# Experts' outputs returned to their tokens by rows in HBM and indirect transfers instead of by spreading matrices

## The chip, the cores and the metric

The program runs on one core of one Trainium2 chip. The metric is the device time of one execution in microseconds (us), as the median of several runs. The engines are TensorE (PE; its weight loads are shown as PEld), VectorE (DVE), ScalarE (ACT), GpSimd (POOL) and SyncE (SP), which here does nothing but issue the transfers of weights; 16 DMA engines move the data.

## The reference, cut to what matters

The program is two transformer blocks in float32 for 256 tokens of width 1024. The first block has two layers, and the feed-forward part of its second layer is a mixture of eight experts, of which each token takes two. That is the part that the change is about:

```python
def moe_swiglu(h, router, wg, wu, wd):            # h: 256 tokens x 1024, 8 experts, d_ff 3584
    logits = (xt @ router).astype(jnp.float32)
    top_logit, top_e = lax.top_k(logits, TOP_K)   # TOP_K = 2
    gate = jax.nn.softmax(top_logit, axis=-1)
    ...
    def expert_block(args):
        xb, e = args
        return swiglu(xb, wg[e], wu[e], wd[e])    # (silu(x@wg) * (x@wu)) @ wd

    ys = lax.map(expert_block, (xs, blk_e)).reshape(n_slots, d)
    ys = ys * slot_gate[:, None].astype(ys.dtype)
    out = jax.ops.segment_sum(ys, slot_tok, num_segments=n_tok + 1)[:n_tok]
    return out.reshape(b, s, d)
```

So each token's result is the sum of two experts' rows, each times its gate, and it is added to the residual x. The second block then starts with a norm of x.

## The kernel before, in words

The whole program is written out by hand, one instruction stream for each engine, with semaphores between them. A token block is 128 tokens, so x is a tile `xv` of 128 partitions by two token blocks (q = 0, 1) by 1024 columns, which stays in SBUF.

**Ahead of the experts** (`moe_sparse` in the streams of TensorE and VectorE). The router's logits give `route`, each token's rank within its experts, and `logit[:, 66:70]`, its two gates. When no expert has over CAP = 96 tokens (else `moe_dense` runs, which did not happen here), VectorE builds 16 pieces of a 0/1 matrix `pick` (L2170), and TensorE multiplies x by it (L1156): 16 banks of 384 columns, each the gathered tokens of four experts for one chunk of 128 columns of x. VectorE takes each bank to `big` (L2191) and copies the first expert's tokens to `hcur` (L2194). In between it builds a second set of 16 pieces, `weigh` (L2176): for each expert, token by slot, with the gate as its value. Behind the 16 gathering banks TensorE transposes `weigh` in four banks of four (L825), and VectorE copies them out (L2198) into `back`, slot by token. The two PSUM banks `pt` are used in turn, and a bank is filled again only when VectorE has emptied it.

**One expert.** Its weights come as 46 tiles: gate and up in two parts of 512x4 and 384x4 columns (tiles "g", "u", part 0 and 1, eight tiles each), then down in two halves of the output (h = 0, 1), seven tiles each. SyncE issues them in that order into ten slots (six of `ring`, and `xc`, `biasb` and two halves of `prob`), each when TensorE has freed its slot, which makes it run up to ten tiles ahead. A group of 96 tokens is three groups of 32, and TensorE's array is used as four column strips of 32, the fourth taking a piece of the others' work; each instruction of L1098 (gate, up) and L1124 (down) handles one strip. At the end of each half of down ScalarE copies partitions of the result (L1690) and VectorE adds the fourth strip's part to them (`add_sides`, L2232 to L2237), which gives `ysum[:, h, :]`, 96 slots by 512 columns.

**Back to the tokens.** `spread_out(h, nth)` (L1141 to L1146) multiplies `backcur`, the current expert's 128x256 piece of `back`, by `ysum[:, h, :]`: two matmuls of 128x512, one for each token block, into the banks `po` and `pada`. VectorE adds both to x (`add_spread`, L2206). There are 17 of them: the one of h = 0 stands inside the same expert's second half of down, behind its second tile; the one of h = 1 stands in the next expert's first gate part, behind its second tile (the first expert has one too, of zeros); the last expert's stands behind the loop, between the turns of the context.

**Behind the experts.** The second block's first steps are TensorE's turning of the context tokens (`turn_context`, L1137), VectorE's `take_context` (L2160), TensorE's first projection of the context, "c4" (L852), then the turning of x by `turner` (L833), the projection "c0" (L852) and the ones of x. The norm of x needs `x_ready`: ScalarE squares x (L1551), VectorE and ScalarE make the root, and VectorE makes `turner` (L1831), on which L833 waits.

GpSimd has nothing in the experts' stage. It waits for a free slot to prepare a table for the last attention (L743 on), which is used far later.

## Time and profile before

| | us |
|---|---|
| median of 3 runs (2952.91 to 2957.2) | 2956.97 |
| profiled execution, its own time | 2956.31 |
| its span, from the first to the last instruction | 2954.5 |

In the profiled execution TensorE is busy 94% of the span, its weight loads 59%, VectorE 43%, ScalarE 15%, GpSimd 2%. The chain of waits that ended last lies on TensorE for 88% of the span, on VectorE for 7%, on "issue" for 2%, on DMA, GpSimd and ScalarE for 1% each. The span in 40 slices of 74 us looks so, with the busy share in tenths, the clock that was granted to TensorE (9 is full, 2.4 GHz; the other level is 1.2 GHz), and the rate of the DMA:

```
PE   7889999989799999999999998899979999988998
PEclk9889999969799999999999999999999999999999
GB/s 269 187 172 143 172 168 175 200 172 101 171 338 378 358 395 376 377 385 362 392 382 353 395 223 83 67 114 172 171 72 114 171 172 128 61 79 47 163 166 99
```

The stretch at 338 to 395 GB/s is the experts' stage. A busy share says which engine works, not which one is waited for; that is read from timelines and waits in the stretch that is asked about. In a timeline a row merges instructions of one line that follow each other; "x" is how many, and what stands in square brackets is the idle time ahead and who ended it. A float32 matmul is recorded as two passes, so counts on TensorE are twice the number of instructions.

### The profile page before, as it was taken

The numbers are of one execution on the slowest core, as the hardware profiler recorded it, in microseconds if no ns is written. First come the engines' busy times: TensorE is split into PE (matmuls) and PEld (weight loads), VectorE is DVE, ScalarE is ACT, GpSimd is POOL, SyncE is SP. The second block draws the span as 40 slices with busy tenths as digits, with TensorE's granted clock in tenths as the row PEclk, the third lists the DMA queues.
The fourth block names the chain that finished last, engine by engine and source line by source line (L and its number), as shares of the span: only waits on it lengthen the run. The fifth ranks groups of instructions, "written<-read, shape, count | busy, mean of one in ns | idle before, by whom it ended". The sixth has DMA issues, their size and how long they took to land.

```text
span 2954.5 us, 49536 instructions
## 1 busy us (share of the span) xinstructions
...
## 2 busy tenths in 40 slices
PE   7889999989799999999999998899979999988998
...
PEclk9889999969799999999999999999999999999999
...
GB/s 269 187 172 143 172 168 175 200 172 101 171 338 378 358 395 376 377 385 362 392 382 353 395 223 83 67 114 172 171 72 114 171 172 128 61 79 47 163 166 99
DMA packets 309636, 629.79 MB, mean 213 GB/s; under 512 B 14841, under 2 KB 197505, under 8 KB 292912
## 3 DMA queue, kind: packets, MB, share of 16 engines
...
## 4 chain that ended last, share of the span: by engine, by line
PE 88%; DVE 7%; issue 2%; DMA 1%; POOL 1%; ACT 1%; DVEq 0%; POOLq 0%; SPq 0%; ACTq 0%
PE pacc L1024 13%; PE pt L852 10%; PE pacc L1098 10%; PE pt L1098 7%; PE pt L1024 6%; PE pacc L1062 5%; PE pacc L1124 5%; PE pt L1124 5%; PE pacc L965 5%; PE po L1098 3%; PE pt L1062 3%; PE pt L1003 2%; PE pt L1361 2%; DVE prob L1914 2%; PE pacc L875 1%
## 5 line engine op out<-in xcount | busy, mean ns | idle before, releaser
L2218 DVE TENSOR_TENSOR gateb<-kT,pt 128x512 f32<-128x512 f32 (+1 forms) x32 | 19.9, 621 | 452.4 <-PE pt L1098 451.7
L852 PE MATMUL pt<-ring,hT 128*128 128x256 f32 (+1 forms) x896 | 206.6, 391 | 7.9 <-ACTq L1572 3.9
L852 PEld LDWEIGHTS pt<-ring,hT 128*128 128x128 f32 x896 | 174.6, 205 | 37.0 <-issue 13.9
L1098 PE MATMUL pacc<-ring,bigc 128*32 128x512 f32 (+1 forms) x1920 | 190.3, 550 | 4.4 <-issue 3.2
L1024 PE MATMUL pacc<-probT,prob 128*128 128x128 f32 x1440 | 170.6, 275 | 0.0
L1024 PEld LDWEIGHTS pacc<-probT,prob 128*128 128x128 f32 x1440 | 165.6, 192 | 0.0
L1098 PEld LDWEIGHTS pacc<-ring,bigc 128*32 128x32 f32 x1920 | 63.1, 110 | 128.2 <-issue 128.2
L1098 PE MATMUL pt<-ring,bigc 128*32 128x512 f32 (+1 forms) x1280 | 138.3, 550 | 0.0
L1124 PE MATMUL pacc<-ring,bigc 128*32 128x512 f32 x864 | 137.9, 595 | 0.0
L1062 PE MATMUL pacc<-prob,chunks 128*128 128x512 f32 x282 | 136.3, 592 | 0.0
L1124 PE MATMUL pt<-ring,bigc 128*32 128x512 f32 x1056 | 126.6, 593 | 0.0
L2028 DVE TENSOR_TENSOR prob<-ring 128x512 f32<-128x512 f32 x86 | 59.5, 692 | 153.8 <-PE pacc L1024 107.1
L1609 ACT ACTIVATE prob<-prob,den 128x256 f32<-128x256 f32 (+3 forms) x192 | 99.2, 518 | 156.5 <-DVEq L1942 152.6
L965 PE MATMUL pacc<-ring,hT 128*128 128x512 f32 x256 | 111.3, 593 | 0.9 <-DVEq L2014 0.9
L852 PE MATMUL pt<-ring,prob 128*128 128x256 f32 x448 | 103.0, 390 | 5.5 <-DVEq L2163 4.0
L2455 DVE SCALAR_TENSOR_TENSOR bigc<-big,convw,bigc 128x256 f32<-128x256 f32 x240 | 100.3, 480 | 4.4 <-DVE hid L2501 0.5
L825 PE MATMUL pt<-const,prob 128*128 128x128 f32 (+1 forms) x448 | 71.1, 303 | 31.4 <-DVEq L1802 28.0
L1682 ACT ACTIVATE kT<-pacc 128x512 f32<-128x512 f32 (+1 forms) x48 | 26.1, 545 | 502.0 <-PE pacc L1098 502.0
L852 PEld LDWEIGHTS pt<-ring,prob 128*128 128x128 f32 x448 | 86.8, 195 | 19.8 <-issue 6.1
L1062 PEld LDWEIGHTS pacc<-prob,chunks 128*128 128x128 f32 x282 | 53.6, 190 | 67.4 <-issue 67.4
L1098 PEld LDWEIGHTS pt<-ring,bigc 128*32 128x32 f32 x1280 | 41.6, 110 | 82.1 <-issue 82.1
L1024 PE MATMUL pacc<-hT,ring 128*128 128x128 f32 x736 | 89.7, 275 | 0.0
...
## 6 DMA issues: line engine op xcount, KB each, us to landing
ring<-in_moe_w_down SPq DMA_DIRECT2D x80, 1024.0 KB, 14.0
ring<-in_w_gate_up SPq DMA_DIRECT2D x66, 1024.0 KB, 5.1
ring<-in_w_ada SPq DMA_DIRECT2D x48, 1024.0 KB, 5.7
ring<-in_moe_w_gate SPq DMA_DIRECT2D x48, 1024.0 KB, 5.4
ring<-in_moe_w_up SPq DMA_DIRECT2D x48, 1024.0 KB, 14.5
ring<-in_w_down SPq DMA_DIRECT2D x33, 1024.0 KB, 4.9
ring<-in_moe_w_gate SPq DMA_DIRECT2D x32, 768.0 KB, 9.4
ring<-in_moe_w_up SPq DMA_DIRECT2D x32, 768.0 KB, 6.5
```

The source lines that it names most:

```text
L825: return pe.transpose(dst, src, ident[0:n, 0:n])
L852: ins = pe.matmul(t[:, q * 256:q * 256 + n], src[:, k, q * P:q * P + P], w[:, k, 0:n], start=(k == 0), stop=(k == KC - 1))
L965: ins = pe.matmul(pacc[:, o:o + 512], src[:, kc, q * P:q * P + P], w[:, k, h * 512:h * 512 + 512], start=(kc == 0), stop=(kc == KC - 1))
L1003: ins = pe.matmul(pt[cc][:, j * S + lo:j * S + lo + P], tiles[j][:, k, cc * P:cc * P + P], half(k, q), start=(k == 0), stop=(k == KC - 1))
L1024: ins = pe.matmul(bank_[:, o:o + P], left(k), right(k), start=(k == 0), stop=(k == 3))
L1062: ins = pe.matmul(down_bank[m][:, 0:512], left[m], right[m], start=(g == 0), stop=(g == groups - 1), skip_group_check=True)
L1098: ins = pe.matmul(((X, Y, Z) if kind == "g" else up_bank)[r][32 * j:32 * j + 32, 0:w], hcurv[:, kc, 32 * g:32 * g + 32], moe_view(tile_)[: ...
L1124: ins = pe.matmul(banks[0 if j < 3 else i][32 * j:32 * j + 32, :], actT[:, f, 32 * g:32 * g + 32], w[:, f - 4 * t, :], start=(t == 0 and ( ...
L1361: ins = pe.matmul(t[:, h * S + lo:h * S + hi], w[:, k, h * P:h * P + P], hTv[:, k, lo:hi], start=(k == 0), stop=(k == KC - 1))
L1609: act.activation(prob[:, o:o + b.nk], prob[:, o:o + b.nk], ACT.Exp, scale=-1.0, bias=den[:, 8 + (i % 4) * 4 + j:9 + (i % 4) * 4 + j], accu ...
L2028: go(ve.tensor_tensor(s1, a21, a22, ALU.add))
L2455: go(ve.scalar_tensor_tensor(out=y[:, cc, :], in0=src, scalar=wk, in1=y[:, cc, :], op0=ALU.mult, op1=ALU.add))
```

## The change

There are no spreading matrices any more: `weigh`, `back`, `backcur`, the transposes, `spread_out` and `add_spread` are gone. `add_sides` now copies three strips rather than two, and adds three. When half h of expert e is in `ysum`, GpSimd writes its 96 rows of 512 columns to a tensor in HBM, `expert_rows` (768 rows of 1024), and waits for that transfer before it allows the next copy into `ysum` (`y_free`, which starts at 2, so that the two halves alternate). VectorE works out the row that each token has with each of its experts (`find_rows`, six small steps behind the first expert's tokens). Behind the last write GpSimd issues four indirect transfers, one for each token block and choice, each of 128 rows of 4 KB, into `big`, and VectorE multiplies each by its gate and adds it to x (four passes over 128x1024), behind `take_context`. `x_ready` is told one token block at a time.

```diff
@@ -739,6 +736,21 @@
             for dst, src in pos_loads:
                 pool.dma_start(dst, src, allow_slow_non_contiguous=True).then_inc(positions, 16)
             pool.sem_inc(slot_free[7], 1)
+            pool.sem_inc(y_free, 2)
+            for e in range(NE):
+                for h in range(2):
+                    pool.wait_ge(y_copied, e * 2 + h + 1)
+                    pool.wait_ge(y_ready, e * 6 + 9 + 3 * h)
+                    pool.dma_start(expert_rows[e * CAP:e * CAP + CAP, 512 * h:512 * h + 512], ysum[0:CAP, h, :])\
+                        .then_inc(y_written, 16)
+                    pool.wait_ge(y_written, 16 * (2 * e + h + 1))
+                    pool.sem_inc(y_free, 1)
+            pool.wait_ge(rows_wanted, 1)
+            for q in range(QT):
+                for c in range(2):
+                    j = 2 * q + c
+                    pool.indirect_dma_start(big[:, j * D:j * D + D], None, expert_rows,
+                                            bass.IndirectOffsetOnAxis(ap=top_i[:, j:j + 1], axis=0)).then_inc(rows_back[q], 16)
...
 
-            def spread_out(h, nth):
-
-                pe.wait_ge(spread_taken, nth)
-                for q, bank_ in enumerate((po, pada)):
-                    ins = pe.matmul(bank_[:, :], backcur[:, q * P:q * P + P], ysum[:, h, :], start=True, stop=True)
-                ins.then_inc(spread_done, 1)
-
...
@@ -1157,33 +1162,19 @@
                                             pick[:, q, half * 4 * CAP:(half + 1) * 4 * CAP],
                                             start=(q == 0), stop=(q == QT - 1))
                         ins.then_inc(filled, 1)
-                pe.wait_ge(weighed_out, 1)
-                for e in range(0, NE, 2):
-                    t, filled, uses, emptied = bank()
-                    pe.wait_ge(emptied, uses)
-                    for k in range(4):
-                        ins = transpose(t[:, k * P:k * P + P], weigh[:, e + k // 2, k % 2, :])
-                    ins.then_inc(filled, 1)
...
                 for e in range(NE):
                     pe.sem_inc(wide_filled, 14)
                     pe.wait_ge(h_current, e + 1)
-                    pe.wait_ge(y_ready, e * 4 + 2)
-
-                    def last_spread():
-                        pe.wait_ge(y_ready, e * 4 + 4)
-                        spread_out(1, e * 2 + 1)
+                    pe.wait_ge(y_ready, e * 6 + 3)
...
-                    def nothing():
-                        pass
-
-                    gate_up(e, "g", 0, None, [nothing, last_spread])
-                    pe.wait_ge(spread_taken, e * 2 + 2)
+                    gate_up(e, "g", 0, None, [])
+                    pe.wait_ge(y_ready, e * 6 + 6)
...
@@ -1199,16 +1190,12 @@
                         down(e, 0, t, (X, Y, Z))
                     down(e, 1, 0, (pt[0], pt[1], turned), freed(("d", 0, 6, 0)))
                     down(e, 1, 1, (pt[0], pt[1], turned))
-                    pe.wait_ge(back_current, e + 2)
-                    pe.wait_ge(y_ready, e * 4 + 6)
-                    spread_out(0, e * 2 + 2)
                     for t in range(2, 7):
                         down(e, 1, t, (pt[0], pt[1], turned))
                     pe.drain().then_inc(freed(("d", 1, 6, 0)), 1)
                 turn_context(0, (0, 1))
                 turn_context(1, (0,))
-                pe.wait_ge(y_ready, NE * 4 + 4)
-                spread_out(1, NE * 2 + 1)
+                pe.wait_ge(y_ready, NE * 6 + 6)
                 turn_context(1, (1,))
...
@@ -1687,7 +1674,8 @@
                         act.wait_ge(wide_taken, e * 14 + (j + 1))
                     for h in range(2):
                         act.wait_ge(y_done, e * 2 + (h + 1))
-                        act.activation(ysum[:, h, :], (X, pt[0])[h][:, :], ACT.Copy).then_inc(y_copied, 1)
+                        act.wait_ge(y_free, e * 2 + (h + 1))
+                        act.activation(ysum[0:CAP, h, :], (X, pt[0])[h][0:CAP, :], ACT.Copy).then_inc(y_copied, 1)
...
             def moe_sparse():
                 g = colA[:, COL["ffn_norm_g"] + KC:COL["ffn_norm_g"] + 2 * KC]
                 for e in range(NE):
@@ -2170,20 +2172,11 @@
                         go(ve.tensor_scalar(pick[:, q, e * CAP:e * CAP + CAP], cst("iota")[:, 0:CAP], r,
                                             den[:, 2 + q:3 + q], ALU.is_equal, ALU.mult))
                 tell(picked)
-                for e in range(NE):
-                    for q in range(QT):
-                        r = route[:, 16 + q * NE + e:17 + q * NE + e]
-                        go(ve.tensor_scalar(weigh[:, e, q, :], cst("slots"), r,
-                                            logit[:, 80 + q * NE + e:81 + q * NE + e], ALU.is_equal, ALU.mult))
-                tell(weighed_out)
                 go(ve.memset(ysum[:, 1, :], 0.0))
                 go(ve.memset(stage, 0.0))
-                go(ve.memset(backcur, 0.0))
                 settle()
-                ve.sem_inc(back_current, 1)
-                ve.sem_inc(y_ready, 4)
+                ve.sem_inc(y_ready, 6)
                 ve.sem_inc(turned_taken, 1)
-                ve.sem_inc(spread_taken, 1)
...
@@ -2192,22 +2185,7 @@
                                             t[:, 0:4 * CAP].rearrange("p (e n) -> p e n", e=4), g[:, k:k + 1], None, ALU.mult))
                         tell(emptied)
                 ve.tensor_copy(hcur, gathered[:, 0, :]).then_inc(h_current, 1)
-                for e in range(0, NE, 2):
-                    t, filled, uses, emptied = bank()
-                    ve.wait_ge(filled, uses)
-                    go(ve.tensor_copy(back[:, e * S:(e + 2) * S], t[:, :]))
-                    tell(emptied)
-
-                def add_spread(h, nth):
-
-                    ve.wait_ge(spread_done, nth)
-                    for q, bank_ in enumerate((po, pada)):
-                        o = x[:, q * D + 512 * h:q * D + 512 * h + 512]
-                        ins = ve.tensor_tensor(o, o, bank_[:, :], ALU.add)
-                        if q == 0:
-                            ins.then_inc(y_shifted, 1)
-                        else:
-                            ins.then_inc(spread_taken, 1)
+                find_rows()
...
@@ -2229,17 +2207,17 @@
                 def add_sides(e, h, banks):
 
                     ve.wait_ge(y_done, e * 2 + (h + 1))
-                    ve.tensor_copy(yside[32:64, h, :], banks[1][96:128, :]).then_inc(y_shifted, 1)
-                    ve.tensor_copy(yside[64:96, h, :], banks[2][96:128, :]).then_inc(y_shifted, 1)
+                    for g in range(3):
+                        ve.tensor_copy(yside[32 * g:32 * g + 32, h, :], banks[g][96:128, :]).then_inc(y_shifted, 1)
                     ve.wait_ge(y_copied, e * 2 + (h + 1))
                     ve.wait_ge(y_shifted, e * 6 + (3, 6)[h])
-                    for lo in (32, 64):
+                    for lo in (0, 32, 64):
                         ve.tensor_tensor(ysum[lo:lo + 32, h, :], ysum[lo:lo + 32, h, :], yside[lo:lo + 32, h, :], ALU.add)\
                           .then_inc(y_ready, 1)
 
                 def expert(e, last=False):
-                    add_spread(1, e * 2 + 1)
-                    ve.tensor_copy(backcur, back[:, bass.ds(e * S, S)]).then_inc(back_current, 1)
+                    if last:
+                        ve.sem_inc(rows_wanted, 1)
...
@@ -2255,7 +2233,6 @@
                         ve.tensor_copy(hcur, big[:, bass.ds((e + 1) * EW, EW)]).then_inc(h_current, 1)
                     take_turned(e, 5)
                     add_sides(e, 0, (X, Y, Z))
-                    add_spread(0, e * 2 + 2)
                     if last:
                         context_scales()
                     add_sides(e, 1, (pt[0], pt[1], turned))
@@ -2264,13 +2241,19 @@
                     expert(e)
                 expert(NE - 1, last=True)
                 take_context(0)
-                add_spread(1, NE * 2 + 1)
                 take_context(1)
-                ve.wait_ge(y_shifted, NE * 6 + 1)
-                ve.wait_ge(spread_taken, NE * 2 + 2)
-                ve.sem_inc(x_ready, QT)
+                for q in range(QT):
+                    ve.wait_ge(rows_back[q], 32)
+                    for c in range(2):
+                        w = logit[:, 66 + 2 * c + q:67 + 2 * c + q]
+                        link(ve.scalar_tensor_tensor(out=xv[:, q, :], in0=big[:, (2 * q + c) * D:(2 * q + c + 1) * D],
+                                                     scalar=w, in1=xv[:, q, :], op0=ALU.mult, op1=ALU.add))
+                    ve.sem_inc(x_ready, 1)
+                ve.sem_inc(vector_chain, 32)
+                chain[0] += 32
 
```

(Left out: names of semaphores and buffers that come or go, the constant `slots`, `find_rows` itself, and the counts that `moe_dense` keeps in step.)

In the order of TensorE's stream, the seam of two experts reads so before (the last tiles of the second half of down, then the first gate part; `chunks` holds `ysum`, `kT` holds `backcur`, `bigc` the tokens and the hidden values):

```order
L1124 MATMUL pacc<-ring,bigc 32x512
L1124 MATMUL pt<-ring,bigc 32x512 x11
L1124 MATMUL pacc<-ring,bigc 32x512
L1098 MATMUL pacc<-ring,bigc 32x512 x24
L1145 MATMUL po<-chunks,kT 128x512
L1145 MATMUL pada<-chunks,kT 128x512
L1098 MATMUL pacc<-ring,bigc 32x512 x48
L1098 MATMUL pacc<-xc,bigc 32x512 x12
L1098 MATMUL pacc<-biasb,bigc 32x512 x12
```

and now:

```order
L1136 MATMUL pacc<-ring,bigc 32x512
L1136 MATMUL pt<-ring,bigc 32x512 x11
L1136 MATMUL pacc<-ring,bigc 32x512
L1110 MATMUL pacc<-ring,bigc 32x512 x72
L1110 MATMUL pacc<-xc,bigc 32x512 x12
L1110 MATMUL pacc<-biasb,bigc 32x512 x12
L1110 MATMUL pt<-prob,bigc 32x512 x8
L1110 MATMUL po<-prob,bigc 32x512 x4
```

The pair that writes `po` and `pada` is gone, and the gate's tiles on both sides of it follow each other. The other pair of an expert, behind the second tile of down's second half, goes in the same way.

VectorE ahead of the first expert before (`probT` is `weigh`, `kT` is `back`):

```order
L2170 TENSOR_SCALAR qT<-const,route,den 128x96 x16
L2176 TENSOR_SCALAR probT<-const,route,logit 128x128 x16
L2179 MEMSET chunks 128x512
L2180 MEMSET qT 128x512
L2181 MEMSET kT 128x256
L2191 TENSOR_SCALAR big<-pt,colA 128x4x96 x16
L2194 COPY bigc<-big 128x768
L2198 COPY kT<-pt 128x512 x4
```

and now:

```order
L2172 TENSOR_SCALAR qT<-const,route,den 128x96 x16
L2175 MEMSET chunks 128x512
L2176 MEMSET qT 128x512
L2184 TENSOR_SCALAR big<-pt,colA 128x4x96 x16
L2187 COPY bigc<-big 128x768
L2158 TENSOR_TENSOR work<-const,logit 128x32
L2160 TENSOR_TENSOR work<-work,route 128x32
L2161 TENSOR_REDUCE work<-work 128x4
L2162 SCALAR_TENSOR_TENSOR work<-logit,work 128x4
L2164 TENSOR_SCALAR work<-work 128x4
L2165 CAST top_i<-work 128x4
```

The 16 pieces of `weigh` between `pick` and the gathering banks are gone, and behind the copy of the first expert's tokens the four copies of `back` are replaced by the six steps of `find_rows`.

VectorE behind the last expert before, from its last `add_sides` on (`prob` is the context's tile):

```order
L2232 COPY work<-pt 32x512
L2233 COPY work<-pacc 32x512
L2237 TENSOR_TENSOR chunks<-chunks,work 32x512 x2
L2160 TENSOR_SCALAR prob<-pacc,gsc,mod 128x128 x8
L2206 TENSOR_TENSOR x<-x,po 128x512
L2206 TENSOR_TENSOR x<-x,pada 128x512
L2160 TENSOR_SCALAR prob<-pacc,gsc,mod 128x128 x8
```

and now, with GpSimd's new instructions below it:

```order
L2211 COPY work<-pt 32x512 x2
L2211 COPY work<-pacc 32x512
L2215 TENSOR_TENSOR chunks<-chunks,work 32x512 x3
L2148 TENSOR_SCALAR prob<-pacc,gsc,mod 128x128 x16
L2249 SCALAR_TENSOR_TENSOR x<-big,logit,x 128x1024 x4
```

```order
L737 DMA posi<-in_positions 15x1
L744 DMA expert_rows<-chunks 96x512 x16
L752 DMA big<-expert_rows,top_i 128x1024 x4
L755 MEMSET biasb 16x889
L758 DMA biasb<-in_na_rpb 16x7x31
L761 ISA
```

The adds to x stood between the two halves of `take_context`; now they are four wider passes behind both, and they read `big`, which the four indirect transfers fill. Those stand behind the 16 writes in GpSimd's queue, and its old work (`biasb`) behind them.

## Rows read from the trace of the kernel before

**Rows 1.** Stages of the span: us, busy time of each engine, granted clock, DMA share, GB/s.

```profile
747.00:802.50 55.50, 37.45 (x122) 24.92 (x121) 29.25 (x87) 1.86 (x3) 0.00 (x0) 0.71 0.42 174
802.50:1738.00 935.50, 932.29 (x9064) 310.36 (x9064) 129.28 (x258) 116.30 (x189) 3.86 (x3) 1.00 0.97 370
```

**Rows 2.** Timeline, TensorE, the start of one expert.

```profile
1153.57 5.36 PE L1098 MATMUL pacc<-ring,bigc 128*32 128x512 f32 x48 [0.44 <-issue]
1158.85 1.12 PE L1145 MATMUL po<-chunks,kT 128*128 128x512 f32 x2
...
1160.77 10.51 PE L1098 MATMUL pacc<-ring,bigc 128*32 128x512 f32 x96
```

**Rows 3.** Groups by line in the experts' stage: the spreading matmuls.

```profile
L1145 PE MATMUL po<-chunks,kT 128*128 128x512 f32 x34 | 19.1, 645 | 0.0
```

**Rows 4.** DMA issues at 1156.4 to 1157.0 and at 1207 to 1208, us to landing.

```profile
ring<-in_moe_w_up SPq DMA_DIRECT2D x1, 1024.0 KB, 16.9
...
prob<-in_moe_w_up SPq DMA_DIRECT2D x1, 768.0 KB, 5.1
```

**Rows 5.** Stretches of five microseconds inside one expert.

```profile
1120.00:1125.00 5.00, 5.00 (x47) 1.51 (x43) 1.17 (x4) 0.00 (x0) 0.00 (x0) 1.00 1.05 387
...
1135.00:1140.00 5.00, 5.00 (x36) 1.46 (x28) 1.00 (x2) 0.00 (x0) 0.00 (x0) 1.00 0.76 222
1140.00:1145.00 5.00, 5.00 (x49) 1.59 (x52) 1.28 (x2) 0.00 (x0) 0.00 (x0) 1.00 0.67 228
...
1160.00:1165.00 5.00, 5.00 (x42) 1.33 (x45) 1.49 (x3) 0.00 (x0) 0.00 (x0) 1.00 1.01 424
```

**Rows 6.** Timeline of TensorE and VectorE ahead of the first expert.

```profile
769.40 4.29 PE L1156 MATMUL pt<-qT,x 128*128 128x384 f32 x8 [6.13 <-DVEq L1802]
769.43 4.19 DVE L2176 TENSOR_SCALAR probT<-const,route,logit 128x128 f32<-128x128 f32 x16 [0.15 <-DVE qT L2170]
...
776.37 21.39 PE L1156 MATMUL pt<-qT,x 128*128 128x384 f32 x56 [2.69 <-DVEq L1802]
...
788.76 0.62 DVE L2191 TENSOR_SCALAR big<-pt,colA 128x384 f32<-128x384 f32 x1 [0.67 <-PE pt L1156]
...
798.56 0.56 DVE L2194 COPY bigc<-big 128x768 f32<-128x768 f32 x1
...
802.54 1.02 PE L1098 MATMUL pacc<-ring,bigc 128*32 128x512 f32 x5 [1.22 <-DVEq L1802]
```

**Rows 7.** Two stretches at the lower clock.

```profile
776.00:779.00 3.00, 2.63 (x4) 1.51 (x5) 0.88 (x2) 0.00 (x0) 0.00 (x0) 0.50 0.00 0
...
1749.00:1751.00 2.00, 2.00 (x6) 1.53 (x6) 0.67 (x4) 1.31 (x4) 0.00 (x0) 0.50 0.44 135
```

**Rows 8.** Timeline behind the last expert.

```profile
1738.09 0.69 DVE L2232 COPY work<-pt 32x512 f32<-32x512 f32 x1 [7.83 <-PE pacc L1124]
...
1747.92 1.06 ACT L1551 ACTIVATE prob<-x 128x1024 f32<-128x1024 f32 x1 [9.14 <-DVEq L2271]
1747.94 8.83 PE L852 MATMUL pt<-ring,prob 128*128 128x256 f32 x32 [3.99 <-DVEq L2163]
...
1749.89 0.29 DVE L1831 TENSOR_SCALAR turner<-const,den 128x128 f32<-128x128 f32 x1 [0.36 <-ACT den L1557]
...
1756.61 3.73 PE L833 MATMUL pacc<-turner,x 128*128 128x128 f32 x32
...
1760.18 7.07 PE L852 MATMUL pt<-ring,prob 128*128 128x256 f32 x32
```

**Rows 9.** DMAs issued by GpSimd, KB each, us to landing.

```profile
biasb<-skew_scratch POOLq DMA_DIRECT2D x64, 64.0 KB, 2.4
skew_scratch<-biasb POOLq DMA_DIRECT2D x1, 3556.0 KB, 38.8
...
biasb<-in_na_rpb POOLq DMA_DIRECT2D x1, 13.6 KB, 5.2
```

**Rows 10.** VectorE groups by shape: one pass over 1024 columns.

```profile
L2578 DVE SCALAR_TENSOR_TENSOR bigc<-pt,bigc 128x1024 f32<-128x1024 f32 x2 | 2.4, 1224 | 4.9 <-PE pt L1377 4.9
```

42 lines of the change are left out of this document (28 added, 14 removed).

## The prediction, made before the changed kernel was run

> **What bounds the kernel now.** I read the stages first, then the timeline of each place that the change touches, then the DMA. In the experts' stage, from 802.5 to 1738.0, TensorE is busy 932.29 of 935.5 us at the full clock, 2.4 GHz [rows 1]. Eight experts in 935.5 us are 116.9 us each, and what TensorE does there is the stage. VectorE (129 us) and ScalarE (116 us) have long pauses in it, so what they gain or lose inside the stage costs nothing by itself. Ahead of it, from 747.0 to 802.5, TensorE is busy 37.45 of 55.5 us at a mean clock of 0.71 [rows 1]: there it waits, for VectorE. The one resource near TensorE in the experts' stage is the DMA, with a share of 0.97 [rows 1]. So three questions decide: what TensorE's stream gets shorter by, whether the weights still come in time, and what the way through HBM costs behind the last expert, where nothing of the experts' stage covers it.
>
> **The change part by part.**
>
> *The spreading matmuls.* In the first gate part a pair goes from 1158.85 to the next tile's first matmul at 1160.77: 1.92 us. The two tiles before it take 5.28 us from 1153.57, where the four behind it take 10.51 with the end of the last one in it, so 5.2 by their rate [rows 2]; the array changes from four strips to one block and back, and I take 2.0 us for each pair. The group by line has 34 records of the `po` half, at two for each matmul 17 pairs [rows 3]. 16 stand inside the stage: 16 x 2.0 = 32 us. The seventeenth stands behind the loop, where VectorE sets the pace; it is worth nothing.
>
> *What hides the rest inside the stage.* VectorE has four passes of 128x512 less per expert and four of 32x512 more, ScalarE copies 96 partitions rather than 128 at the same length: both in their pauses. TensorE now waits for both halves' `y_ready` ahead of the second gate-or-up part, 20 us behind the last tile of down, where three copies and three adds of 0.7 us are long done (one copy is in [rows 8]). ScalarE's wait for `y_free` is for a write issued over 90 us earlier. If a write took so long, the next y copy would wait and TensorE with it; the slowest transfer of GpSimd's queue, 3556 KB, took 38.8 us [rows 9].
>
> *The weights.* An expert is now 116.9 - 4.0 = 112.9 us long. Does the DMA deliver 44.0 MB in that? Its 14 tiles of down (14.7 MB) come at 387 GB/s, where the share is full, those of gate and up (29.4 MB) at 424, of which I take 418: 37.9 + 70.2 = 108.1 us [rows 5]. The new writes are 0.39 MB per expert, 1.0 us at 387. 109.1 of 112.9 us: it fits, with 3.8 us left. The queue says the same. The longest time to landing is 16.9 us, for the tile issued at 1156.5, that is 1173.4; it is the eleventh tile of the expert that starts at 1153.57, and with 5.36/2 = 2.6 us per tile and the pair TensorE comes to it at 1181 [rows 2, 4]. That leaves 8 us, and 6 without the pair. 50 us later a tile lands in 5.1 us [rows 4], so the queue has run dry again and nothing adds up from expert to expert. And from 1135 to 1145 the share is 0.76 and 0.67 at 222 and 228 GB/s [rows 5], since SyncE waits there for slots. So I cost the weights at nothing.
>
> *Ahead of the first expert.* VectorE builds `weigh` from 769.43 to 773.62 and then clears three buffers; TensorE fills two banks by 773.69 and is idle for 2.69 us until 776.37, since nobody empties them [rows 6]. Behind that pause its clock is 1.2 GHz, 0.50 at 776 to 779 [rows 7]. The 14 other banks take 21.39 us, to 797.76, of which the later ones go at 0.62 + 0.67 = 1.29 us each [rows 6]. Now VectorE is ready after two clearings, before the first bank is full, and TensorE does not pause. At the full clock the 14 banks are 14 x 1.29 = 18.1 us, from 773.7 to 791.8: 6.0 us earlier. The copy to `hcur` ended at 799.12, 1.36 us behind the gathers' end, and the first expert started only at 802.54, since the transposes and four copies of `back` stood between; now it can start 0.3 us behind the copy, at 793.4. Sum: 802.5 - 793.4 = 9.1 us. If the clock falls all the same, the pause (2.7) and the wait behind the copy (3.1) are what is won, 5.8 us. I take 9.1, since the fall came behind a pause that goes. `find_rows` is six steps on 32 columns, some 1.5 us, and VectorE is next wanted some 40 us later.
>
> *Behind the last expert.* The last tile is done at 1738.09, on the clock of before. Three copies and three adds of 0.7 us: `ysum` is complete at 1742.4 rather than 1741.0. `take_context` then needs no pause for the adds to x (two of 0.68), so c4 starts as before, at 1747.94, and ends at 1756.6, when TensorE wants x turned. In the kernel before `turner` was made from 1749.89 on, so x came with 6 us to spare [rows 8]. What it now takes:
> the write, 192 KB, issued at 1742.5. The trace has 2.4 us for 64 KB and 5.2 for 13.6 KB while weights were streaming [rows 9]; the streaming goes on to about 1750, where the share is down at 0.44 [rows 7], so 5.5: 1748.1.
> The four gathers of 512 KB. None is in the trace. From below: 2.1 MB at 387 GB/s are 5.4 us, and behind them the 2.4 us of a small transfer. From above: at the rate of GpSimd's only large transfer, 3556 KB in 38.8 us, they take 22.9 us [rows 9]. The weights' burst is over by 1750, and rows of 4 KB are long, so I go near the lower end, with 1.2 us on GpSimd for each: block 0 at 1754.5, block 1 at 1756.9.
> The four passes: 1.22 us for a SCALAR_TENSOR_TENSOR of 1024 columns [rows 10], all four ahead of the norm in VectorE's order. Block 0 is added by 1757.0, block 1 by 1759.5; then the root and `turner`, as before 1.1 us behind the first squares. TensorE turns x at 1760.7 rather than 1756.6: 4.1 us. TensorE's pause of 3.99 us at 1744 was followed by a clock of 0.50 at 1749 to 1751 [rows 7, 8], and c4's 32 records took 8.83 us where c0's 32 took 7.07 [rows 8]; the new pause is as long, so I take another 1.7. Sum: 5.8 us lost. Behind it everything is as before: the context's head "c4" and the projection "c0" move with it.
>
> The page DMA: Bandwidth & Descriptors of the Trainium skill (Anatomy of one DMA) gives a GpSimd transfer 2.0 us plus its bytes at 436 GB/s. This trace agrees for the 64 KB (2.15 against 2.4) and not for the 13.6 KB under load (2.03 against 5.2). By that rule x would be turned in time and this loss would be nothing; that is my third case below, whose numbers come from the rows.
>
> *Sum*, against the profiled execution's 2956.3: - 32 - 9.1 + 5.8 = - 35.3, so 2921.0. The median shown is 0.7 above that execution; I leave that in the range.
>
> **The rivals.**
> 1. *The weights become the bound.* For it: a DMA share of 0.97 in the stage [rows 1], of which by this count only 3.5 us per expert are free, and the writes take 1.0 of them. Then an expert gets shorter by 2.5 rather than 4 us, 20 for the stage: 2956.3 - 20 - 9.1 + 5.8 = 2933. Against it: at 1207 a tile lands in 5.1 us [rows 4] with a share as high, so the share counts packets that wait for nothing but their own turn.
> 2. *Gathers at the low rate.* They end at 1748.1 + 22.9 = 1771.0, plus 2.4 to land; two passes and the norm behind the last block, 3.6 us more, so x is turned at 1777: 20.4 + 1.7 = 22 us lost: 2956.3 - 41.1 + 22 = 2937. For it: nothing here shows how long GpSimd needs to read 128 indices and write as many descriptors; its plain issues are much shorter.
> 3. *The way through HBM is hidden.* If write and gathers end by 1752.8, 10.3 us behind 1742.5 (the write at 2.4 and the gathers at 7.8 are 10.2), the four passes and the norm fit ahead of 1756.6 and nothing is lost: 2956.3 - 41.1 = 2915.
> 4. *The clock ahead of the experts falls as before*: 5.8 rather than 9.1: 2924.
> 5. *Slower than before.* One mechanism: GpSimd serves the gathers one by one, index by index, and each is long. The gain is 41.1; it is gone when x is turned later than 1756.6 + 39.4 = 1796.0, so when the gathers take over 1796.0 - 3.6 - 1748.1 = 44 us, 11 us each, for 512 KB (47 GB/s). At 15 us each they are 60, 16 more: 2972. Against it: half the rate of the slowest large transfer in the trace.
> That the change does not do what it says would show as banks over 96 tokens, the other branch; the inputs are those of the trace, and it took this one.
>
> **How the numbers follow.** The forecast (2917 to 2927, with rival 4 in it) 0.50; rival 1 0.12; rival 2, anything between 2927 and 2943, 0.14; rival 3 0.17; slower 0.04; gains that nearly cancel 0.03. What a measurement of this kernel can tell from no change is about 0.2%, 6 us. Faster by more: 0.93; within: 0.03; slower: 0.04. The range from 2912 to 2938 leaves out the slow cases and the far end of rival 2, some 0.12 to 0.15.
>
> **What the profile will show.** Right: an expert's period of 112.9 us with TensorE busy throughout; the first expert 9 us earlier with no stretch at 0.5 in the gathers; behind c4 a pause of TensorE of about 4 us that ends with `turner`, itself behind GpSimd's transfers. Wrong: pauses of TensorE for tiles of weights inside the stage (rival 1); a pause behind c4 of 20 us (rival 2) or none (rival 3); a wait of ScalarE for `y_free` that reaches TensorE would be something I have excluded.

## The result and the profile after

| us | before | changed |
|---|---|---|
| median | 2957.09 (2952.91 to 2957.35, 4 runs) | 2923.11 (2916.54 to 2925.3, 4 runs) |
| profiled execution, its own time | 2956.31 | 2925.3 |
| its span | 2954.5 | 2923.5 |

The ratio is 0.9885, 95% interval 0.9871 to 0.9899: 1.15% faster. The time lies 2 us above the forecast of 2921, so the case forecast as likeliest is the one that came. The two medians differ by 34.0 us. The two profiled executions differ by 31.0 us where the sum said 35.3, so by their traces the sum is off by 4.3 us. The tail alone is off by 5.9; the other terms came out 1.6 us better than forecast. That the median lies closer than that is luck: the profiled execution of the changed kernel is the slowest of its four.

Read in the order of the prediction, first the stages of the changed kernel (us, busy time of PE, PEld, DVE, ACT, POOL, granted clock, DMA share, GB/s), as [rows 1, 7]:

```profile
793.60:1696.20 902.60, 899.49 (x9000) 318.20 (x9000) 128.79 (x254) 116.27 (x189) 7.74 (x15) 1.00 1.00 387
...
776.00:779.00 3.00, 3.00 (x11) 1.81 (x10) 1.32 (x3) 0.00 (x0) 0.00 (x0) 1.00 0.02 5
```

The experts' stage is 902.6 us long rather than 935.5, and TensorE is busy in all but 3.1 us of it. The DMA share has gone from 0.97 to 1.00, which looks like a bound. The waits of TensorE in that stage say that it isn't; here is the whole list:

```profile
PE pacc L1110 <- issue: 3.1, 7, 0.4
PE pacc L1110 <- DVE bigc L2187: 1.4, 1, 1.4
```

No wait names a DMA. The tiles do land later than before, as the page's list of DMA issues shows (median us from issue to landing; before, this one stood at 14.5):

```profile
ring<-in_moe_w_up SPq DMA_DIRECT2D x48, 1024.0 KB, 16.6
```

Ahead of the first expert, the timeline that answers to [rows 6]:

```profile
765.74 3.93 DVE L2172 TENSOR_SCALAR qT<-const,route,den 128x96 f32<-128x96 f32 x16 [1.17 <-issue]
769.78 22.42 PE L1161 MATMUL pt<-qT,x 128*128 128x384 f32 x64 [6.13 <-DVEq L1790]
...
793.00 0.56 DVE L2187 COPY bigc<-big 128x768 f32<-128x768 f32 x1
...
793.62 11.79 PE L1110 MATMUL pacc<-ring,bigc 128*32 128x512 f32 x108 [1.41 <-DVE bigc L2187]
```

All 64 records of the gathering matmuls are one row: no pause, and a clock of 1.00 (2.4 GHz) at 776 to 779 where it was 0.50 (1.2 GHz) [rows 7]. A stretch at 0.50 is still there at the start, from 769 to 772; it follows the 6.13 us in which TensorE waits for the pick, as before. The first expert starts 0.6 us behind the start of the copy to `hcur`.

And the tail, which answers to [rows 8]:

```profile
1696.24 1.42 DVE L2211 COPY work<-pt 32x512 f32<-32x512 f32 x2 [5.32 <-PE pacc L1136]
...
1701.15 0.51 POOL L744 DMA_DIRECT2D expert_rows<-chunks  x1 [17.51 <-DVE chunks L2215]
1703.49 2.64 DVE L2148 TENSOR_SCALAR prob<-pacc,gsc,mod 128x128 f32<-128x128 f32 x8 [0.22 <-DVE prob L2148]
...
1707.42 1.19 PE L864 MATMUL pt<-ring,prob 128*128 128x256 f32 x2 [5.60 <-issue]
1708.20 1.03 POOL L752 DMA_INDIRECT big<-expert_rows,top_i  x1 [6.54 <-DMA expert_rows<-chunks]
1709.54 0.99 POOL L752 DMA_INDIRECT big<-expert_rows,top_i  x1 [0.30 <-issue]
...
1710.67 8.84 PE L864 MATMUL pt<-ring,prob 128*128 128x256 f32 x30 [2.07 <-issue]
...
1716.38 5.89 DVE L2249 SCALAR_TENSOR_TENSOR x<-big,logit,x 128x1024 f32<-128x1024 f32 x4 [10.25 <-DMA big<-expert_rows,top_i]
...
1724.02 0.29 DVE L1819 TENSOR_SCALAR turner<-const,den 128x128 f32<-128x128 f32 x1 [0.36 <-ACT den L1544]
...
1724.37 5.84 PE L845 MATMUL pacc<-turner,x 128*128 128x128 f32 x32 [4.86 <-DVE turner L1819]
...
1730.05 1.25 PE L864 MATMUL pt<-ring,prob 128*128 128x256 f32 x5
```

The reader is to follow one thing down this list: nobody else is late. y is complete at 1700.6, GpSimd's write holds its gathers until 1708.20, the gathers hold VectorE until 1716.38, VectorE's four passes hold `turner` until 1724.02, and TensorE, which was done with its tile (c4) at 1719.5, waits 4.86 us for it. The chain of waits names the same links; two of its pieces (start, length) are the two transfers:

```profile
1701.15 6.21 DMA expert_rows<-chunks
...
1709.54 6.82 DMA big<-expert_rows,top_i
```

Absolute times can't be compared across the stage, so I count from T0, the end of the last tile of `down` (1738.09 before, 1696.24 after). The projection c0 starts at T0 + 22.1 before [rows 8] and at T0 + 33.8 after: 11.7 us lost.

The whole account of the two spans: the part up to the pick, 765.36 against 765.74, + 0.4; from the pick to the first expert, 37.18 against 27.88, - 9.3; the stage, 935.55 against 902.62, - 32.9; T0 to c0, + 11.7; the remainder - 0.9. Sum - 31.0, the difference of the spans.

### The profile page after: what moved, and what is told of

It reads as the page before. It is cut to its first block, busy times and chain, and to the rows that moved or that the text cites. A ratio compares the mean times of both kernels' runs of the same rounds, so it can differ in the third digit from the quotient of the medians.

```text
span 2923.5 us, 49387 instructions
## 1 busy us (share of the span) xinstructions
PE 2745.3 (94%) x20781; PEld 1749.9 (60%) x20781; DVE 1276.1 (44%) x3088; ACT 437.5 (15%) x1031; POOL 85.8 (3%) x118
## 4 chain that ended last, share of the span: by engine, by line
PE 87%; DVE 7%; issue 2%; DMA 1%; POOL 1%; ACT 1%; PEld 0%; PEldq 0%; DVEq 0%; POOLq 0%; SPq 0%; ACTq 0%
PE pacc L1036 13%; PE pt L864 10%; PE pacc L1110 10%; PE pt L1110 7%; PE pt L1036 6%; PE pacc L1074 5%; PE pacc L1136 5%; PE pt L1136 5%; PE pacc L977 4%; PE po L1110 3%; PE pt L1074 3%; PE pt L1015 2%; PE pt L1348 2%; DVE prob L1902 2%; PE pacc L887 1%
## 5 line engine op out<-in xcount | busy, mean ns | idle before, releaser
L864 PEld LDWEIGHTS pt<-ring,hT 128*128 128x128 f32 x896 | 174.7, 205 | 37.2 <-issue 14.0
L864 PEld LDWEIGHTS pt<-ring,prob 128*128 128x128 f32 x448 | 87.2, 197 | 24.3 <-issue 10.5
```

What stands on the lines that cost most here:

```text
L864: ins = pe.matmul(t[:, q * 256:q * 256 + n], src[:, k, q * P:q * P + P], w[:, k, 0:n], start=(k == 0), stop=(k == KC - 1))
```

## The experiments

Besides its time, each run's own timeline is used: the length from the pick (the first row on `qT`) to the first expert, the stage, and the tail from T0. That is needed because the part of the program that the change doesn't touch moved the pick's start between 761.2 and 769.2 us from profile to profile, more than most of the terms in question.

**The head alone.** The kernel before, without `weigh`, its transposes and the copies to `back`, which is cleared; the spreading matmuls stay and spread nothing.

```diff
-                for e in range(NE):
-                    for q in range(QT):
-                        r = route[:, 16 + q * NE + e:17 + q * NE + e]
-                        go(ve.tensor_scalar(weigh[:, e, q, :], cst("slots"), r, ...))
-                tell(weighed_out)
...
-                for e in range(0, NE, 2):
...
-                    go(ve.tensor_copy(back[:, e * S:(e + 2) * S], t[:, :]))
+                link(ve.memset(back, 0.0))
```

> The kernel before without the building of weigh, its 16 transposes and the four copies of back (back is cleared instead, so the spreading matmuls multiply by zeros and the experts' sum is left out of x). Spreading matmuls, adds and the end stay. Theory: this part alone gives the 9.3 us that the trace of the changed kernel shows ahead of the first expert, so 9 us less than before (2948), with no stretch at the lower clock inside the gathering matmuls. Rival: a part of the 9.3 us was another run's clock; then 6 us less (2951).

Measured: 2944.61 us (2941.55 to 2948.33), ratio to the kernel before 0.995 (0.9931 to 0.9969), that is 9 to 20 us less; 9.3 lies at the near end of that. The trace holds the size of the part in question:

```profile
767.34 3.92 DVE L2163 TENSOR_SCALAR qT<-const,route,den 128x96 f32<-128x96 f32 x16 [1.17 <-issue]
771.38 22.38 PE L1156 MATMUL pt<-qT,x 128*128 128x384 f32 x64 [6.13 <-DVEq L1795]
795.17 5.36 PE L1098 MATMUL pacc<-ring,bigc 128*32 128x512 f32 x48 [1.42 <-DVE bigc L2181]
```

From the pick to the first expert 27.83 us rather than 37.18: the 9.3 us of the changed kernel come with these edits alone.

**The pairs alone.** The kernel before with 15 of its pairs of spreading matmuls left out (their sums never reach x).

```diff
                 pe.wait_ge(spread_taken, nth)
+                if 1 < nth <= NE * 2:
+                    pe.sem_inc(spread_done, 1)
+                    return
```

> The kernel before without 15 of the 16 pairs of spreading matmuls inside the experts' stage (all but the first; the experts' sum in x is wrong for it); everything else, the adds by VectorE too, stays. Theory: TensorE is the bound and a pair costs 2.06 us, so 15 x 2.06 = 31 us less than before (2926), all of it between the first expert's start and the last one's end. Rival: the DMA of weights takes over with a free time of only 3.5 us per expert; without the HBM writes that would give up to 8 x 3.5 = 28 us, with pauses of TensorE for tiles.

Measured: 2928.51 us (2925.61 to 2929.31), ratio 0.9896 (0.9877 to 0.9914). In its timeline the stage goes from the second of these rows to the third:

```profile
779.82 19.72 PE L1159 MATMUL pt<-qT,x 128*128 128x384 f32 x56 [2.67 <-DVEq L1805]
804.32 1.92 PE L1098 MATMUL pacc<-ring,bigc 128*32 128x512 f32 x16 [1.22 <-DVEq L1805]
...
1708.99 0.69 DVE L2235 COPY work<-pt 32x512 f32<-32x512 f32 x1 [4.92 <-PE pacc L1124]
```

904.67 us for 935.55: 30.9 for 15 pairs, 2.06 each. The changed kernel's 32.9 are 16 of them. Nothing else in the stage gained or lost. The head here is that of the kernel before, yet its 56 records took 19.72 us where [rows 6] have 21.39: the same code, pause and fall of the clock, but the clock came back sooner. So 1.7 of the 9.3 us won in the head vary from execution to execution. The tail varies as well. This run has the tail of the kernel before, in which the context's tile c4 took 8.83 us [rows 8], and here it took 10.04, with the clock at 0.50 from 1719 to 1723, so c0 starts at T0 + 23.3 instead of + 22.1:

```profile
1718.86 10.04 PE L852 MATMUL pt<-ring,prob 128*128 128x256 f32 x32 [4.01 <-DVEq L2166]
```

**The head's gain taken apart.** VectorE's 16 routing steps put back into the changed kernel.

```diff
+                for e in range(NE):
+                    for q in range(QT):
+                        r = route[:, 16 + q * NE + e:17 + q * NE + e]
+                        go(ve.tensor_scalar(probT[:, ...], cst("iota"), r, ..., ALU.is_equal, ALU.mult))
```

> The changed kernel with VectorE's 16 routing rows built again between the pick and the clearing of big, where the kernel before built them (into probT, which nothing reads then); all else is as changed. Before, those 16 steps and the transposes and copies behind them lay between the pick and the gathering matmuls, and left TensorE a pause after which 64 matmuls began at clock 0.50. Theory: the clock falls when the pause returns. The gathering matmuls start about 4.5 us later than in the changed kernel's 769.8 and run with a stretch at clock 0.50, so the first expert starts 6 to 7 us later, and the time is about 2930 us (6 to 7 over the changed kernel's 2923). Rival: the pause of 4.2 us by itself costs its own length and no more, and the fall of the clock in the kernel before came from TensorE's transposes and waits that this kernel doesn't have: 2927 us, and the granted clock stays at 1.00 in the gathering matmuls.

Measured: 2926.62 us (2925.22 to 2929.63), ratio 0.9894 (0.9877 to 0.991).

```profile
766.48 3.93 DVE L2172 TENSOR_SCALAR qT<-const,route,den 128x96 f32<-128x96 f32 x16 [1.17 <-issue]
770.52 4.30 PE L1161 MATMUL pt<-qT,x 128*128 128x384 f32 x8 [6.13 <-DVEq L1790]
...
776.81 20.02 PE L1161 MATMUL pt<-qT,x 128*128 128x384 f32 x56 [1.99 <-DVEq L1790]
...
798.25 10.08 PE L1110 MATMUL pacc<-ring,bigc 128*32 128x512 f32 x92 [1.42 <-DVE bigc L2192]
```

```profile
776.00:779.00 3.00, 2.19 (x4) 1.27 (x5) 1.23 (x2) 0.00 (x0) 0.00 (x0) 0.65 0.00 0
```

The pause is back (1.99 us) and with it the low clock, 0.65 at 776 to 779; the two parts of the gathers take 24.3 us where they took 22.4 in one piece. The first expert starts 31.77 us behind the pick instead of 27.88: 3.9 us, 2.0 of pause and 1.9 of clock. The mechanism is that of the theory (the rival has the clock at 1.00), the size that of the rival: I had reckoned 6 to 7, with gathers that start 4.5 us later. They start 4.04 us behind the pick here as in the changed kernel; only the third bank waits. What is left of the head's gain, 31.77 against 35.5 and 37.2 in the two kernels that build and copy `back`, is 3.7 to 5.4 us for its transposes and copies and for the third clearing.

**Is the DMA share of 1.00 a bound?** In the changed kernel each half of y is written more often, for experts 0 to 6: nine times in one run, four times in another.

```diff
                     pool.dma_start(expert_rows[...], ysum[0:CAP, h, :]).then_inc(y_written, 16)
+                    for i in range(8 if e < NE - 1 else 0):
+                        pool.dma_start(more_rows[i * CAP:i * CAP + CAP, :], ysum[0:CAP, h, :]).then_inc(y_extra, 16)
+                    pool.wait_ge(y_extra, 16 * 8 * min(2 * e + h + 1, 2 * (NE - 1)))
```

> The changed kernel with each half of y written nine times instead of once for experts 0 to 6 (the eight extra copies go to a tensor that nobody reads): 3.1 MB more on the DMA engines per expert. At 387 GB/s that is 8.1 us per expert. Theory of the prediction: an expert needs 109.1 us of transfers in 112.9 us, so 3.8 us are free and 4.3 us show per expert: 7 x 4.3 = 30 us, about 2953 us. Rival A: the weights bound the changed kernel already (no reserve, since its DMA share reads 1.00 in the stage): 7 x 8.1 = 57 us, about 2980 us. Rival B: the reserve is larger than 8 us, since the share reads full only because transfers are queued ahead: no change, 2924 us.

> As the run with nine writes of each half of y, but four: three extra copies for experts 0 to 6, 1.2 MB more or 3.0 us at 387 GB/s per expert. The run with nine cost 30 us in the stage of the eight experts, as a reserve of 3.8 us per expert would have it. Theory: 3.0 us lie inside the reserve, no change: 2923 us. Rival: the cost is linear from the first transfer on (3.7 us per expert for 8.1): 7 x 1.6 = 11 us, 2934 us.

Measured: nine writes 2955.36 us (2949.66 to 2962.38, 10 runs), ratio 0.9992 (0.9979 to 1.0004); four writes 2923.09 us (2916.48 to 2931.28), ratio 0.9892 (0.9862 to 0.9922). The stage is 902.8 us long with four writes (902.6 with one) and 932.0 with nine. TensorE's waits in it, with nine (us in total, times, longest; each row of this kind has these three):

```profile
PE pt L1141 <- DMA ring<-in_moe_w_down: 7.6, 6, 1.7
PE pacc L1115 <- DMA xc<-in_moe_w_gate: 4.4, 6, 0.8
...
PE pt L1115 <- DMA prob<-in_moe_w_up: 3.3, 7, 0.9
...
```

and with four, all of them:

```profile
PE pacc L1115 <- issue: 3.2, 7, 0.5
PE pacc L1115 <- DVE bigc L2192: 1.4, 1, 1.4
```

An extra 3.0 us of transfers per expert cost nothing; an extra 8.1 cost 29.4 / 7 = 4.2. The reserve is 8.1 - 4.2 = 3.9 us per expert, where the prediction had 3.8 by bytes over rate. That rests on 387 GB/s for the extra bytes. With nine writes the stage's mean rate is 398 GB/s, at which they take 7.9 us and the reserve is 3.7. The runs themselves say only that it lies between 3.0 and 8.1; the exact place assumes that each us beyond it costs one. With nine the tail is 3.7 us longer as well (c0 at T0 + 37.5), which covers the rest of its median. Both rivals of the run with nine fall, and so does the linear one of the run with four: the share of 1.00 hid a reserve of about the size counted.

**The way through HBM left out.** The changed kernel with its four gathers issued ahead of the last expert, from a weight tensor instead of the rows (x gets the wrong rows).

```diff
+                if e == NE - 1:
+                    fetch()
...
-            for q in range(QT):
-                for c in range(2):
-                    j = 2 * q + c
-                    pool.indirect_dma_start(big[...], None, expert_rows, ...)
```

> The changed kernel with the four gathers issued at the last expert's start, from a weight tensor with rows of the same length (so x gets rows of weights in place of the experts'), and not behind the last write; the writes, the gathers and the four passes are all still made. Theory: what the end costs (11.7 us until the first projection of x) is the time of write and gathers on the path; without it x is ready when VectorE's passes are done, at 18 us behind the last tile, where c4 ends as well: 10 to 11 us less than the changed kernel, 42 less than before (2914 to 2916). Rival: the pauses of TensorE ahead of and inside c4 (5.6 and 2.1 us put down to issue) cost it; then they stay, and it is 4 to 6 us less than the changed kernel (2918).

Measured: 2917.11 us (2914.44 to 2919.88), ratio 0.9857 (0.9838 to 0.9876).

```profile
1706.44 1.19 PE L869 MATMUL pt<-ring,prob 128*128 128x256 f32 x2 [5.58 <-issue]
1711.81 9.12 PE L869 MATMUL pt<-ring,prob 128*128 128x256 f32 x30 [4.17 <-issue]
1720.77 3.73 PE L850 MATMUL pacc<-turner,x 128*128 128x128 f32 x32
1724.34 5.99 PE L869 MATMUL pt<-ring,prob 128*128 128x256 f32 x27
```

With T0 at 1694.91, c0 starts at + 29.4: 4.4 us sooner than in the changed kernel, 7.3 later than before. x is ready in time now (there is no idle time ahead of L850), yet most of the tail's loss stays: TensorE comes late by itself, with two pauses that the profile puts down to issue. The size is the rival's: the median is 6.0 us below the changed kernel's, 4.4 of them in the tail. The transit and these pauses lie side by side; taking one away uncovers the other.

**Do GpSimd's transfers make the pauses?** As the run before, and the last half of y isn't written either.

```diff
+                    if (e, h) == (NE - 1, 1):
+                        break
                     pool.dma_start(expert_rows[e * CAP:e * CAP + CAP, 512 * h:512 * h + 512], ysum[0:CAP, h, :])\
```

> As the run whose gathers were issued ahead from a weight tensor, and in addition the last expert's second half of y isn't written at all, so GpSimd moves nothing behind the last expert; rows of the last expert are missing from the output. That run still had two pauses that the profile gives to issue, 5.6 us ahead of TensorE's context tile (L864 of the changed kernel) and 4.2 us inside it, where the kernel before had one of 4.0. Theory: these pauses are TensorE waiting for its own instructions, which the DMA engines bring late because GpSimd's transfer and the weight tiles lie ahead of them: without the write there is one pause of about 4 us again, the tile ends 3 to 5 us earlier, and the time is 2913 us. Rival: they belong to where the instructions lie in the program (the same in both kernels): both pauses stay, 2917 us.

Measured: 2915.81 us (2914.75 to 2918.33), ratio 0.9854 (0.9838 to 0.9871).

```profile
1710.90 1.19 PE L871 MATMUL pt<-ring,prob 128*128 128x256 f32 x2 [5.63 <-issue]
1714.22 8.72 PE L871 MATMUL pt<-ring,prob 128*128 128x256 f32 x30 [2.13 <-issue]
1722.78 3.73 PE L852 MATMUL pacc<-turner,x 128*128 128x128 f32 x32
```

Both pauses stand as in the changed kernel (5.60 and 2.07), so the theory that GpSimd's transfers make them falls. With T0 at 1699.69, c0 starts at + 26.7. Why the second pause was 4.17 in the run before this one, where the write was still there, and 2.6 and 2.8 in those with four and nine writes, stays open: whether transfers lengthen it isn't shown.

**Do they belong to a place in TensorE's program?** Four small matmuls and two fulfilled waits ahead, where TensorE idles anyway.

```diff
                 turn_context(1, (0,))
+                for h in range(2):
+                    pe.wait_ge(y_ready, NE * 6 + 3)
+                    for bank_ in (po, pada):
+                        pe.matmul(bank_[:, 0:16], ident, ident[:, 0:16], start=True, stop=True)
                 pe.wait_ge(y_ready, NE * 6 + 6)
```

> The run without the last write and with its gathers ahead, and in addition four small matmuls (16 columns, into banks that nothing reads then) and two waits that are long fulfilled on TensorE, between its context transposes and the wait for y of the last expert, where it idles 1.4 us. The two pauses put down to issue (5.6 us ahead of the context tile L864 and 2.1 us behind its second matmul) stood in that run as in the changed kernel, with and without GpSimd's transfers. Theory: they belong to the place of the instructions in TensorE's program: with four matmuls more ahead the second pause must come at least four matmuls sooner, so ahead of the tile, which then runs in one piece of 32. Rival: they belong to something that the tile waits for (data or a bank), whatever stands ahead: two matmuls, then a pause of 2 us, as before. Theory gives 2913 to 2916 us, the rival 2916.

Measured: 2911.07 us (2910.55 to 2912.67), ratio 0.985 (0.983 to 0.987).

```profile
1706.25 8.77 PE L871 MATMUL pt<-ring,prob 128*128 128x256 f32 x32 [5.59 <-issue]
1714.86 3.73 PE L852 MATMUL pacc<-turner,x 128*128 128x128 f32 x32
1718.43 6.86 PE L871 MATMUL pt<-ring,prob 128*128 128x256 f32 x31
```

Eight records (four matmuls; the expectation's two matmuls ahead of the pause are two records) more ahead, and the second pause is gone; the tile runs as 32 records in one piece, and from T0 (1694.57) c0 starts at + 23.9 instead of + 26.7. Its median is 4.7 us below that of the kernel without the four matmuls, but their ratios to the kernel before, each run beside it, are 0.985 and 0.9854, so the times don't tell the two apart; the traces do. So the second pause depends on what stands ahead in TensorE's program and not on what the tile waits for, as the theory says. Of the 2.8 us in the tail, 2.1 are the pause; the tile's records took 8.8 us instead of 9.9, a size by which they differ between executions of equal code too. In the changed kernel a transfer on the queue for instructions falls into the first pause and another ahead of the end of the second (stretches 1704 to 1705 and 1708 to 1709; packets, MB, share):

```profile
q8 instruction: 1, 0.02, 7.2%
...
q8 instruction: 1, 0.02, 6.9%
```

That TensorE waits for these packets is my reading; the trace doesn't link them. In the run with the four matmuls such a packet comes at 1707 to 1708, inside the tile, and there is no pause, so a packet alone doesn't make one. The first pause is there in every kernel: 3.99 us in [rows 8], where it is named after VectorE. In all of them the tile starts some 4 us behind the later of two events, the end of the context's turning on TensorE and VectorE's first half of `take_context`: 1743.94 to 1747.94 before, 1703.27 to 1707.42 after, 1702.12 to 1706.25 here. So it isn't a cost of the change; what differs is the event from which it counts.

**Who issues the last write?** The changed kernel with the last write of y on ScalarE's queue.

```diff
+                    act.wait_ge(y_copied, 2 * NE)
+                    act.wait_ge(y_ready, 6 * NE + 6)
+                    act.dma_start(expert_rows[(NE - 1) * CAP:NE * CAP, 512:1024], ysum[0:CAP, 1, :]).then_inc(last_written, 16)
```

> The changed kernel with the last 192 KB write of y issued from ScalarE's queue instead of GpSimd's, as soon as y is complete; GpSimd only waits for it and then issues its gathers. In the changed kernel 7.05 us pass between y's last addition and GpSimd's first gather. Theory: 2.0 to 2.5 of them are GpSimd's own way of issuing a transfer (it builds the descriptors), the rest is the transfer and its receipt behind the weight tiles in the DMA engines' queues: the wait becomes 4.5 to 5.5 us and the time 2921 us. Rival: all of it is the transfer behind the weight tiles, whoever issues it: 7.0 us again and 2923 us.

Measured: 2922.99 us (2918.13 to 2924.7), ratio 0.9877 (0.986 to 0.9895).

```profile
1701.21 0.33 ACTq L1758 DMA_DIRECT2D expert_rows<-chunks  x1
...
1708.69 1.03 POOL L756 DMA_INDIRECT big<-expert_rows,top_i  x1 [24.54 <-DMA expert_rows<-chunks]
```

From y's last sum to the first gather it is 7.6 us here and 7.6 in the changed kernel; from the issue 7.5, against 7.05 from GpSimd (the expectation took the 7.05 for the first of the two). The rival is right: the wait isn't GpSimd's way of issuing. How much of it is transfer behind weight tiles and how much receipt isn't separated by this run.

**The hybrid.** Experts 0 to 6 go through HBM, and their rows are gathered and added during the last expert, where VectorE and the DMA engines have room; the last expert alone is added by two pairs of spreading matmuls, as before.

```diff
-            for e in range(NE):
+            for e in range(NE - 1):
...
+                go(ve.tensor_scalar(weigh[:, q, :], cst("iota")[:, 0:CAP], route[:, 23 + q * NE:24 + q * NE],
+                                    logit[:, 87 + q * NE:88 + q * NE], ALU.is_equal, ALU.mult))
...
+                        add_rows()
...
+                add_spread(1, 2)
```

> The changed kernel with the last expert returned by spreading matmuls as before (two pairs, two transposes) and the gathers of the seven others issued and added during the last expert. Theory: the end costs what it did before, the head and the stage keep their gain but for one pair and two transposes (2.7 us): 9.3 + 32.9 - 2.7 = 39.5 us less than before (2917), 6 to 8 less than the changed kernel. Rival: the gathers and passes hold up VectorE or the weights during the last expert, TensorE pauses there, and it is no faster than the changed kernel.

Measured: 2918.38 us (2911.33 to 2919.66), ratio 0.9866 (0.9848 to 0.9884). The changed kernel's interval touches that, so both were run again side by side on one chip.

> The changed kernel as it is, once more, beside the hybrid on the same chip: 2923 us, ratio to the kernel before 0.988 to 0.989.

> The hybrid once more: experts 0 to 6 written and gathered during the last expert, the last expert added by spreading matmuls. Its first run had the x turned 7.7 us earlier behind the last tile than the changed kernel. Theory: 5 to 7 us less than the changed kernel in the same call, 2917 us. Rival: the two are the same within what is measured (their intervals touched in separate calls).

Measured: the changed kernel 2922.87 us (2921.45 to 2923.56), ratio 0.9888 (0.9868 to 0.9908); the hybrid 2916.17 us (2912.83 to 2916.57), ratio 0.9866 (0.9846 to 0.9886). Their runs don't overlap: the hybrid's median is 6.7 us below the changed kernel's, and it is the fastest here of those that leave nothing out. Its gathers, and then its tail:

```profile
1594.79 1.03 POOL L759 DMA_INDIRECT big<-expert_rows,top_i  x1 [7.43 <-DMA expert_rows<-chunks]
...
1607.47 2.60 DVE L2239 SCALAR_TENSOR_TENSOR x<-big,logit,x 128x1024 f32<-128x1024 f32 x2 [21.10 <-DMA big<-expert_rows,top_i]
```

```profile
1708.15 9.57 PE L871 MATMUL pt<-ring,prob 128*128 128x256 f32 x32 [3.87 <-issue]
1717.56 3.73 PE L852 MATMUL pacc<-turner,x 128*128 128x128 f32 x32
1721.13 7.07 PE L871 MATMUL pt<-ring,prob 128*128 128x256 f32 x32
```

c0 starts at T0 (1696.99) + 24.1, against + 33.8 and + 32.5 in the two profiles of the changed kernel, and its stage is 2.6 us longer (905.2): 5.8 to 7.1 us, which is what the times say. Beside the stream of weights its first rows take 12.7 us to come (1594.79 to 1607.47) instead of 8.2. VectorE waits for them, TensorE doesn't: its waits in this stage are the two of the changed kernel, with no transfer among them. The rerun of the changed kernel shows the other side of the variation, too: its gathering matmuls took 23.97 us instead of 22.42, with the clock at 0.55 rather than 0.89 from 772 to 776, and its first expert came 29.42 us behind the pick. No pause lies in them; the low clock that every profile has at their start lasted longer.

## Why the prediction held, step by step

- *The spreading matmuls*: 32 predicted, 32.9 measured; 2.06 us for a pair and not 2.0, shown twice, with the pairs alone and with all of the change.
- *The cover inside the stage*: no wait for `y_ready` or `y_free` appears on TensorE in the stage. Held.
- *The weights*: at nothing, right, and for the reason given: reserve 3.8 by the count, 3.7 to 3.9 by the two runs with more writes. Rival 1 is out.
- *Ahead of the first expert*: 9.1 predicted, 9.3 measured in the two profiles compared. Over all profiles the head took 35.5 and 37.2 us as it was before and 27.8 to 29.4 as changed, so the gain is 6.1 to 9.4. The step's mechanism is shown by the run with the 16 steps put back; its split between pause, clock and copies was a little off (the clock's share is 1.6 to 3.3 us and depends on the execution). Rival 4 is out: in none of eleven profiles without the pause does the clock fall a second time. In one of them the low clock at the start lasted 1.5 us longer. The sign "no stretch at 0.5 in the gathers" was too strong, since that stretch at the start is in every profile.
- *Behind the last expert*: this term was mis-sized, 11.7 against 5.8. By the sum's own pieces, counted from T0:

| from T0, us | predicted | measured |
|---|---|---|
| y complete | 4.3 | 4.4 |
| write landed, first gather issued | 10.0 | 12.0 |
| first block of x complete in `big` | 16.4 | 20.1 |
| four passes done | 21.4 | 26.0 |
| TensorE turns x | 22.6 | 28.1 |
| c0 starts | 27.9 | 33.8 |

x is turned 5.5 us later than forecast, and four pieces carry it. "The write, 192 KB, ... 5.5" (1.9 of the 5.5): 7.6 us from y's last sum to the first gather, of which 0.5 pass before the issue, 6.2 are transfer and 0.8 lie between landing and gather. I took the price from two small loads into SBUF [rows 9]; this is a write to HBM beside three weight tiles issued within 1.2 us of T0. What of the two makes it longer isn't separated. The gathers "at 1754.5" (1.7): 8.2 us from the first issue to the first block instead of 6.4, and 6.6 to 8.2 in the six profiles with this tail. The "1.2 us on GpSimd for each" had no row behind it; the gathers follow each other by 1.24 to 1.34 us. (The upper price in rival 2 should be 22.3 us and not 22.9 by its own row, which changes nothing.) The four passes (0.9): three took 1.28 us each where I had 1.22, and the last 1.83 (shortest, median and longest, ns):

```profile
L2249 DVE SCALAR_TENSOR_TENSOR x<-big,logit,x x4: 1283/1284/1826, 1716.4 to 1720.5; 128x1024 f32<-128x1024 f32 x4
```

The row I took the price from [rows 10] reads one operand from PSUM, this one reads both from SBUF. The long last pass is in all eight profiles in which GpSimd works on `biasb` beside the passes (1719.18 to 1722.73 here), 1.72 to 2.05 us, and in none of the three others, which have 1.28 to 1.29 throughout; that the two belong together is not tested by a run of its own. Last, the norm (0.9): `turner` is used 2.1 us behind the last pass and not 1.2.

In the changed kernel this chain sets all of the 11.7: x is turned 9.6 us later from T0 than before, and the low clock behind the wait adds 2.1. Taking the transit away gives only 7.1 of them back, since TensorE's own lateness in c4 lies beside it. The tile starts at T0 + 11.2 instead of 9.9, since VectorE's first half of `take_context` is done 1.4 us later behind the third copy and add; it has the second pause, 2.1; and its records take 10.0 us instead of 8.8. "c4 starts as before, at 1747.94, and ends at 1756.6" was wrong: it ends 4.6 us later, and with no transit at all 4.6 us of the tail are lost (the run without write and gathers, c0 at T0 + 26.7). Of these, 1.2 need not be the change's: the run with the pairs alone has the tail of before and its c4 took 10.04 us. So the forecast sign, a pause of about 4 us behind c4 that ends with `turner`, came true by luck in its size: 4.86, because x and c4 were both about 5 us later than forecast.
- *The clock in the tail*: 1.7 predicted. L845 took 5.84 us against 3.73 in every run in which TensorE didn't wait for `turner`, 2.1 us (1.6 to 3.0 in the six profiles with that wait). The granted clock at 1722 to 1728, the third number from the end, is 0.50, the level of 1.2 GHz:

```profile
1722.00:1728.00 6.00, 3.63 (x17) 3.63 (x18) 3.22 (x12) 1.93 (x5) 0.73 (x1) 0.50 0.00 1
```

The page DMA: Bandwidth & Descriptors of the Trainium skill (Anatomy of one DMA) gives 2.0 us plus the bytes at 436 GB/s for a GpSimd transfer, most of the fixed part being the receipt of the write, heaviest for HBM. For 192 KB that would be 2.5 us, an estimate by that page; this trace has 6.2, so the rule doesn't hold beside a stream of weights. The same page of the Trainium skill (SWDGE vs HWDGE vs iDMA) calls the setup faster from the hardware path; the run with the write on ScalarE's queue shows no gain from it here. The numbers above don't rest on either.

Rival 2 (gathers at 22.9 us) is out: the first pair is there after 8.2 and in this profile the passes over the second follow without a wait. Rival 3 (hidden) is out in the changed kernel, and it is what the hybrid comes near to.
